# The second token half's square sums at four norm boundaries: VectorE adds eight tiles to four, TensorE sums four

## The reference, cut to what matters

```
u = rms_norm(h, norm_g[layer, 0]) * (1.0 + sc1) + sh1
y = hgrn2_mixer(u, ...)            # or dilated_attention_mixer
h = h + (1.0 + g1) * rms_norm(y, norm_g[layer, 1])
u = rms_norm(h, norm_g[layer, 2]) * (1.0 + sc2) + sh2
y = swiglu_ffn(u, ffn_w_in[layer], ffn_w_out[layer])
h = h + (1.0 + g2) * rms_norm(y, norm_g[layer, 3])
```

## Time and profile before

| | before |
|---|---|
| median of 3 runs | 3153.73 us (3150.58 to 3156.85) |
| profiled execution, its own time | 3153.86 us |
| its span | 3152.1 us |
| TensorE busy, matmuls | 3101.5 us, 98% |
| VectorE busy | 1546.5 us, 49% |
| ScalarE busy | 1128.6 us, 36% |
| DMA | 311.77 MB, 99 GB/s on the mean |
| column sums of the boundaries (L2115) | 536 matmul records, 250 ns in the median |

### The profile page before, as it was taken

How to read it: one execution, slowest core, us unless ns; L and a number is a source line. 1 busy time by engine, 2 the same in 40 slices (tenths; PEclk the granted TensorE clock), 3 DMA queues, 4 the chain that set the end, 5 groups by cost and what they waited for, 6 DMA issues and landing times.

```text
span 3152.1 us, 40528 instructions
## 1 busy us (share of the span) xinstructions
PE 3101.5 (98%) x17486; PEld 2594.2 (82%) x17502; DVE 1546.5 (49%) x2113; ACT 1128.6 (36%) x1651; POOL 30.4 (1%) x44
## 2 busy tenths in 40 slices
PE   7999999999999999999999999999999999999999
PEld 6878888888987777988888767888889867798887
DVE  7676654544165645532335654653334654654342
ACT  5555422233233333422224355332222345433231
POOL 0000000000000000000000000000000000000000
PEclk8999999999999999999999999999999999999999
DMA  8433354532232221232222221222322222222222
GB/s 298 147 108 108 108 196 151 192 108 81 94 94 68 67 68 54 78 97 94 94 101 68 67 68 54 81 94 96 105 94 88 68 68 67 76 85 94 99 101 80
DMA packets 211743, 311.77 MB, mean 99 GB/s; under 512 B 9872, under 2 KB 108272, under 8 KB 211568
## 3 DMA queue, kind: packets, MB, share of 16 engines
q1 hardware_dynamic: 200352, 267.14, 25.5%
q0 software_dynamic: 10880, 41.95, 3.8%
q10 hardware_dynamic: 336, 0.12, 0.0%
HBM read 307.06 MB, written 2.10 MB: 98 GB/s over the span
## 4 chain that ended last, share of the span: by engine, by line
PE 90%; DVE 6%; ACT 2%; DMA 1%; issue 1%; ACTq 0%; SPq 0%; POOLq 0%; DVEq 0%
PE G L2019 62%; PE G L2062 9%; PE G L2023 7%; PE X L2115 2%; DVE yT L1551 1%; PE X L2369 1%; PE G L2041 1%; DMA ada_raw<-in_ada_w 1%; DVE acc L1257 1%; PE X L2452 1%; PE G L2169 1%; DVE w_lo L1220 1%; PE X L2436 1%; PE X L2459 1%; PE X L2395 1%
## 5 line engine op out<-in xcount | busy, mean ns | idle before, releaser
L2019 PE MATMUL G<-u_hi,w_hi 128*128 128x512 f32 (+1 forms) x2192 | 882.1, 402 | 7.0 <-DVE w_lo L1220 3.8
L2019 PE MATMUL G<-u_hi,w_lo 128*128 128x512 f32 (+1 forms) x2192 | 857.7, 391 | 0.0
L2019 PE MATMUL G<-u_lo,w_hi 128*128 128x512 f32 (+1 forms) x2192 | 856.2, 391 | 0.0
L1220 DVE TENSOR_TENSOR w_lo<-raw,w_hi 128x2048 fp32r<-128x2048 f32 (+2 forms) x242 | 545.1, 2254 | 505.3 <-ACT w_hi L628 504.8
L628 ACT CAST w_hi<-raw 128x2048 fp32r<-128x2048 f32 (+2 forms) x242 | 454.6, 1880 | 525.9 <-DMA raw<-in_w_ff 240.3
L2019 PEld LDWEIGHTS G<-u_hi,w_hi 128*128 128x128 f32 (+1 forms) x2192 | 409.8, 187 | 117.2 <-issue 25.7
L2019 PEld LDWEIGHTS G<-u_hi,w_lo 128*128 128x128 f32 (+1 forms) x2192 | 409.7, 187 | 93.4
L2019 PEld LDWEIGHTS G<-u_lo,w_hi 128*128 128x128 f32 (+1 forms) x2192 | 410.7, 187 | 83.8 <-issue 1.7
L2019 PE MATMUL G<-ff_hi,w_hi 128*128 128x512 f32 x448 | 174.9, 390 | 0.0
L2019 PE MATMUL G<-ff_hi,w_lo 128*128 128x512 f32 x448 | 174.4, 389 | 0.0
L2019 PE MATMUL G<-ff_lo,w_hi 128*128 128x512 f32 x448 | 174.3, 389 | 0.0
(11 more groups left out here) (419 smaller groups left out, 4405.3 us busy)
## 6 DMA issues: line engine op xcount, KB each, us to landing
raw<-in_w_ff SPq DMA_DIRECT2D x128, 512.0 KB, 4.4
raw<-in_ffn_w_in SPq DMA_DIRECT2D x88, 512.0 KB, 4.4
ada_raw<-in_ada_w POOLq DMA_DIRECT2D x40, 1024.0 KB, 7.2
raw<-in_w_in SPq DMA_DIRECT2D x64, 512.0 KB, 4.3
raw<-in_attn_w_in SPq DMA_DIRECT2D x96, 256.0 KB, 3.7
raw<-in_ffn_w_out SPq DMA_DIRECT2D x40, 512.0 KB, 4.5
raw<-in_hgrn_w_in SPq DMA_DIRECT2D x32, 512.0 KB, 4.6
raw<-in_attn_w_in SPq DMA_DIRECT2D x24, 512.0 KB, 4.3
```

The source lines that it names most:

```text
L1220: tt(w_lo[slot][:, 0:nk, 0:w], raw[slot][:, 0:nk, 0:w], w_hi[slot][:, 0:nk, 0:w].bitcast(F32), ALU.subtract).then_inc(s_lo, 1)
L2019: ins = mm(G[0:c1_ - c0, m, :], w[iw][:, k, c0:c1_], xs[ix][:, x0(b) + kk, :], start=first, stop=last, skip_group_check=True)
```

## The change

At the four boundaries with two norms, and for the second token half only, ScalarE's two squares of h raise a semaphore of their own, s_hsq1. VectorE, behind the first half's last step and ahead of reciprocal(1), waits for both, adds the squares of tiles 4 to 7 onto those of tiles 0 to 3 in place (four tiles of 256 tokens, 128x1024) and raises s_hsum1. TensorE no longer sums behind kk 4. Behind kk 5 it waits for s_hsum1 and sums tiles 0 to 3 for the two blocks of the second half. The first half, the sums of y and the boundaries of the second block stay as they were.

```diff
--- before.py
+++ after.py
@@ -282,6 +282,7 @@
         s_sq, s_sqd, s_std = sem("square_ready"), sem("square_summed"), sem("std_ready")
         s_diag, s_spread = sem("rstd_on_diagonal"), sem("rstd_spread")
         s_yout, s_ysum, s_rstd = sem("half_y_copied"), sem("half_y_summed"), sem("rstd_ready")
+        s_hsq1, s_hsum1 = sem("second_half_h_square_ready"), sem("second_half_h_squares_added")
         s_part, s_first, s_acc, s_mix = sem("half_tile_summed"), sem("first_square_ready"), sem("first_squares_added"), sem("mix_ready")
         s_h, s_n, s_uhi, s_u = sem("h_tile_ready"), sem("normed_tile_ready"), sem("u_hi_ready"), sem("u_ready")
         s_silu, s_ff, s_fhi, s_fr = sem("silu_ready"), sem("hidden_ready"), sem("hidden_hi_ready"), sem("hidden_split")
@@ -717,7 +718,7 @@
                     else:
                         n.take(s_h)
                         k = slice(4 * i, 4 * i + 4)
-                    n.give(sc.activation(tmp[:, k, half[hf]], hT[:, k, half[hf]], ACT.Square), s_sq)
+                    n.give(sc.activation(tmp[:, k, half[hf]], hT[:, k, half[hf]], ACT.Square), s_hsq1 if c0 is not None and hf else s_sq)
 
                 def u_hi_of(hf, k):
                     n.take(s_n)
@@ -1456,6 +1457,9 @@
                             scaled(1, 1)
                             added(1, 1)
                     lower(0, KT - 1)
+                if c0 is not None:
+                    n.take(s_hsq1, 2)
+                    n.give(tt(tmp[:, 0:4, half[1]], tmp[:, 0:4, half[1]], tmp[:, 4:8, half[1]], ALU.add), s_hsum1)
                 reciprocal(1)
                 if c0 is not None:
                     n.own(s_h)
@@ -2133,6 +2137,13 @@
                 if i == 1:
                     n.give(ins, s_sqd)
 
+            def second_h_sums():
+
+                n.take(s_hsum1)
+                for k in range(4):
+                    ins = column_sums(2, tmp[:, k, :], range(2, 4), False)
+                n.give(ins, s_sqd)
+
             def h_sums(hf):
                 for i in range(2):
                     h_part("s", hf, i)
@@ -2188,14 +2199,14 @@
                                     y_sums(1)
                                 elif kk == 1:
                                     spread(1)
-                                elif kk in (4, 5):
-                                    h_part(kind, 1, kk - 4)
+                                elif kk == 5:
+                                    second_h_sums()
                                 elif kk == 6:
                                     spread(1)
                             elif kk == 0:
                                 spread(1)
-                            elif kk in (4, 5):
-                                h_part(kind, 1, kk - 4)
+                            elif kk == 5:
+                                second_h_sums()
                             elif kk == 6:
                                 spread(1)
```

## The result

The changed kernel takes 3167.53 us in the median of six runs (3166.02 to 3171.12), against 3153.39 for the kernel before (3150.58 to 3156.85): a ratio of 1.0046, 95% interval 1.0036 to 1.0056, or +14.1 us. Run once more beside the experiments it was 3166.36 against 3152.27, a ratio of 1.0048 (1.0034 to 1.0061). The forecast was slower, and it is slower, but 3162.7 was named and the range ended at 3167.0, so both the size and the range were missed. The range was missed by 0.5 us only, less than the runs of one kernel differ by; the size, +8.8 us said and +14.1 us measured, was missed by more than that.

The account below looks back on a forecast made before the run. TensorE is busy 98% of the span, but at these boundaries a VectorE-ScalarE-sums chain was taken to bound it. Chain +6.4 and clock +2.4 give +8.8 us on 3153.86, forecast 3162.7 us, range 3156.5 to 3167.

Parts of the forecast that it names:

- What is removed: Sums behind kk 4 at four boundaries: 1.70 us each, hidden before the wait for the last square; chain not shortened.
- The chain: VectorE add between ScalarE's last square and TensorE's sums: +1.25, +2.13, +1.24, +1.77 at boundaries one to four, +6.4 us.
- The waits: TensorE stands still before the sums: 3.5 us instead of 0.54 at the first boundary, 3.3 at the fourth.
- The clock: TensorE's clock falls for one new stretch at second and fourth boundary, none at first and third: +2.4 us.
- one gap of 3.76 us: TensorE gap at 75.61, followed by the 1.2 GHz level; taken as nearest row to the new waits.
- the long low stretch: Low clock begun in the second boundary's first sums (2.77 us against 1.95), still held at 727 to 728, twice as long.
- The signs: Expected in the trace: among others, kk 6 later by 1.2 us (first, third) and 1.8 to 2.1 (second, fourth).
- The price of a stretch: One low-clock stretch: 1.2 us for some 14 slow 256-column matmuls plus 0.35 for the rstd spread, about 1.5 us.
- the prediction's upper bound for the clock: Two low stretches at each of four boundaries, six more than now, less 0.6 us: +8.4 us.
- Longer low stretches: Rival: each boundary gets one low stretch more than before; +11.8 us, 3165.7 us; chance 0.20.
- The other rivals: Chain alone +6.4 us, chance 0.26; chain with old low stretches gone +3.4, 0.10; TensorE the bound -7.0, 0.04.
- The 81 ns: Skill's cost per weight load and matmul: a group of 16 would take an estimated 1.3 us; row shows 1.81.

Follow-up runs that it names:

- The first experiment: Kernel before, sums behind kk 4 removed at the four boundaries, no VectorE add, squares of tiles 0 to 3 left out: 3156.72 us, ratio 1.0024.
- The experiment with the add alone: Kernel before, group behind kk 4 kept, plus a VectorE maximum of tiles 4 to 7 with themselves before the second sums: 3160.96 us, ratio 1.0034.
- filler pair: First and third boundary of the changed kernel with 24 unread 256-column matmuls ahead of TensorE's wait at each of four boundaries: 3158.18 us, 1.0024 to before.
- the steps in kk 6: Kernel before, no add; into mid-kk 6 move the second sums (first, third boundary) or the rstd spread (second, fourth): 3149.46 us, again 3148.22, both 0.9991.

## Why the prediction was wrong

- **What is removed: right.** The group behind kk 4 lay in the shadow of the square. The first experiment took it away alone, and with the clock alike no boundary became shorter (20.07 against 20.11, 17.82 against 17.81).
- **The chain: right.** +6.4 us was the sum, 6.2 was measured, 1.27, 2.04, 1.25 and 1.67 against 1.25, 2.13, 1.24 and 1.77. The experiment with the add alone shows 1.27 and 1.22 at constant clock. That the last u_lo decides at the second and fourth was right too.
- **The waits: right.** 3.58 and 3.29 us where 3.5 and 3.3 were said.
- **The clock: wrong, and this is the step that failed.** The sum took one new low stretch at the second and fourth boundary and none at the first and third, 1.5 us for each, less 0.6 for waits that they hide: "+2.4 us". The traces have 6.8 us of low clock, two such stretches, at every one of the four: 27.3 us against 6.8 before, six stretches more instead of two, and it cost 9.6 us. The likeliest case was read from one gap of 3.76 us, behind which dense matmuls followed; here 16 one-column sums follow. The row nearer to that, the long low stretch from the second boundary's first sums to 728, was used as a bound only. The signs missed with it: kk 6 came 2.9 us later behind T0 at the first boundary, not 1.2, since the slow sums came on top of the chain.
- **The price of a stretch: near on the mean, not at each place.** Six stretches were 8.4 us by the prediction's bound and 9.6 measured, 1.6 us each. It was 1.5 at the second boundary with the add ahead of the last u_lo, 1.2 to 1.3 in the filler pair (2.5 us for two), and 22.31 - 20.07 = 2.2 us in the first experiment. There the sums themselves were slow, 3.42 us for 1.81; the prediction had charged only slow matmuls of 256 columns and the spread behind the sums.
- **What came was the bound, not a rival.** Two stretches at each of the four, six more than before, were the prediction's upper bound for the clock, +8.4; with the chain that is +14.8 (3168.7 us), beside +15.8 at the boundaries. It had no chance of its own and lay outside the range. "Longer low stretches", +11.8 with a chance of 0.20, had the right direction and mechanism, but one stretch more at each boundary, four instead of six.
- **The other rivals fell.** No boundary came through with the low clock of before, and TensorE was never the bound there.

The Trainium skill (TensorE: Matmul & The Clock Gate, "HAM oscillation — how this bites in real kernels") charges half of the throttled time. With the measured 27.3 - 6.8 = 20.5 us more of low clock that gives an estimate of 10.2 us; the boundaries show 9.6. The rule's price agrees with this sum, while single places lie on both sides of it (2.5 us for 6.8 in the filler pair, 2.2 for 3.4 in the first experiment); what was missing in the prediction was how long the clock would be low. The 81 ns that the prediction takes from the same page of the Trainium skill ("Back-to-back issue gap") are stated there for matmuls of 128 columns; the one-column records here stand 113 ns apart (1.81 us for 16), and the forecast didn't use them.

The boundaries lose 15.8 us and the span grew by 12.2. The rest of the profiled execution, whose code is the same, was 3.6 us shorter, and it had 13.8 us less low clock than that of before (41.3 against 55.1 us). In the other kernels this number lies between 38 and 55, so it is scatter between executions. So it is luck that the profiled execution's +12.2 lies nearer to the forecast's +8.8 than the boundaries' +15.8 does. Why it scatters wasn't tried. Nor was it settled what makes one boundary fall and its twin not, as in the filler kernel, nor which share of a fall the wait has and which the thin sums behind it. Thin sums without a wait ahead of them had no fall behind them at the second and fourth boundary of the kernel before.

## What to carry to other kernels

Work taken off the busiest engine is worth nothing where that engine would only wait sooner: find the wait that ends last at that very place, and count what the change adds to its chain. A wait of one or a few microseconds on TensorE with only thin work behind it can be paid again in the clock, by amounts that differ from execution to execution; so cost a lengthened wait with its slow stretches, give the bound that rows show a chance of its own, and include the thin work in the slow part. Moving small steps into the middle of dense work, so that no wait arises, was the only edit here that didn't make the kernel slower, and it probably gained a little (2.6 and 4.1 us in the medians).

## What the runs showed of the hardware

At full clock 16 one-column records hold TensorE for 1.81 us, at the 1.2 GHz level for 3.44: one-column work with its weight loads slows 1.9 times, about as matmuls of 256 columns do (0.12 to 0.213 us from start to start, 1.8 times). Behind waits of 3.3 to 3.7 us and with such sums the clock was low for 6.8 us at seven of eight boundaries in two executions of the changed kernel and for 10.2 us at the eighth; with the same wait of 3.58 us it was 3.4 us at one boundary of the kernel with the add ahead of the last u_lo. A long wait isn't needed: with the sums behind kk 7, the first boundary's clock fell behind waits of 0.70 and 0.46 us with the sums and four matmuls of 128 columns between and behind them, just as a third wait, of 1.79 us, began. Where no wait was over 0.4 us (the steps in kk 6), none of eight boundaries had any low clock. Taking matmuls away made the kernel slower by 5.6 us; adding 96 useless ones to the changed kernel made it faster by 7.
